# One piece of expert weights as nine DMAs instead of one: three w_down pieces at the end of a two-layer encoder

## The reference

```python
def swiglu(t, w_gate, w_up, w_down):
    return (jax.nn.silu(t @ w_gate) * (t @ w_up)) @ w_down

def moe_swiglu(h, w_router, w_gate, w_up, w_down):
    ...
    for e in range(N_EXPERTS):
        ye = swiglu(t, w_gate[e], w_up[e], w_down[e]).astype(jnp.float32)
        out = out + gates[:, e:e + 1] * ye
```

## Time and profile before

| | |
|---|---|
| three executions | 1026.13, 1026.95, 1029.49 us; median 1026.95 us |
| the profiled execution | 1027.61 us |
| its span, first to last instruction | 1024.7 us |
| granted TensorE clock, mean | 0.995 of full speed |
| TensorE busy | 1005.4 us, 98% |
| DMA queue q1 (SP) | 331.64 MB, 82.8% of 16 engines' span |

### The profile page before, as it was taken

How to read it: one execution, slowest core, us unless ns; L and a number is a source line. 1 busy time by engine, 2 the same in 40 slices (tenths; PEclk the granted TensorE clock), 3 DMA queues, 4 the chain that set the end, 5 groups by cost and what they waited for, 6 DMA issues and landing times.

```text
span 1024.7 us, 22739 instructions
## 1 busy us (share of the span) xinstructions
PE 1005.4 (98%) x10130; PEld 572.4 (56%) x10130; DVE 268.6 (26%) x420; ACT 246.2 (24%) x424; POOL 33.7 (3%) x120
## 2 busy tenths in 40 slices
PE   8999999999999899999999999999999999999995
PEld 8987888888898744533334444444444444444331
DVE  7677455554857610000000000000000000000022
ACT  7667434353866200001000000000000000000121
POOL 4000000000101000000000000000000000000010
PEclk9999999999999999999999999999999999999998
DMA  8577665653447999999999999999999999999994
GB/s 282 193 257 250 202 205 168 201 175 111 154 166 289 389 408 419 408 417 418 408 419 416 408 419 415 419 409 416 418 409 419 404 419 409 408 397 418 417 418 167
DMA packets 125744, 346.88 MB, mean 339 GB/s; under 512 B 7224, under 2 KB 42848, under 8 KB 125648
## 3 DMA queue, kind: packets, MB, share of 16 engines
q1 hardware_dynamic: 119632, 331.64, 82.8%
q0 software_dynamic: 3008, 10.40, 3.1%
q10 hardware_dynamic: 3008, 3.42, 0.9%
HBM read 340.71 MB, written 4.72 MB: 337 GB/s over the span
## 4 chain that ended last, share of the span: by engine, by line
PE 90%; DMA 4%; ACT 2%; SPq 2%; DVE 2%; issue 1%; DVEq 0%; ACTq 0%
PE ps L2060 28%; PE ps L2123 14%; PE ps L2071 11%; PE ps L1592 8%; PE ps L1594 8%; PE ps L1593 8%; PE ps L2128 6%; DMA ring<-in_moe_w_down 2%; PE ps L2081 1%; DMA raw_gu<-in_w_out 1%; SPq L885 1%; DMA raw_gu<-in_w_in 1%; PE ps L2157 1%; PE ps L1599 1%; SPq L791 0%
## 5 line engine op out<-in xcount | busy, mean ns | idle before, releaser
L2060 PE MATMUL ps<-ring,xg 128*32 128x512 f32 (+2 forms) x2736 | 315.1, 551 | 0.6 <-ACT xg L1493 0.6
L2123 PE MATMUL ps<-ring,moe_ht 128*32 128x512 f32 x1184 | 149.4, 593 | 1.4 <-DMA ring<-in_moe_w_down 1.4
L2071 PE MATMUL ps<-ring,xg 128*32 128x256 f32 (+2 forms) x2064 | 147.1, 357 | 0.0
L2071 PEld LDWEIGHTS ps<-ring,xg 128*32 128x32 f32 x2064 | 67.1, 110 | 131.4 <-issue 128.6
L2060 PEld LDWEIGHTS ps<-ring,xg 128*32 128x32 f32 x2736 | 86.3, 110 | 77.2 <-issue 44.1
L1592 PE MATMUL ps<-hi_gu,xt_hi 128*128 128x512 f32 (+1 forms) x336 | 125.8, 374 | 0.8 <-DVE lo_gu L2315 0.7
L1594 PE MATMUL ps<-hi_gu,xt_lo 128*128 128x512 f32 (+1 forms) x336 | 123.2, 367 | 0.0
L1593 PE MATMUL ps<-lo_gu,xt_hi 128*128 128x512 f32 (+1 forms) x336 | 123.0, 366 | 0.0
L1475 ACT ACTIVATE moe_silu<-ps 128x512 f32<-128x512 f32 (+2 forms) x24 | 13.4, 557 | 332.4 <-PE ps L2071 274.2
L2770 DVE TENSOR_TENSOR moe_hidden<-moe_silu,ps 128x512 f32<-128x512 f32 (+2 forms) x24 | 15.3, 638 | 242.6 <-PE ps L2071 142.8
L1592 PEld LDWEIGHTS ps<-hi_gu,xt_hi 128*128 128x128 f32 x336 | 63.8, 190 | 12.3 <-issue 1.8
(11 more groups left out here) (345 smaller groups left out, 966.3 us busy)
## 6 DMA issues: line engine op xcount, KB each, us to landing
ring<-in_moe_w_down SPq DMA_DIRECT2D x74, 1024.0 KB, 17.4
ring<-in_moe_w_up SPq DMA_DIRECT2D x59, 1024.0 KB, 17.7
ring<-in_moe_w_gate SPq DMA_DIRECT2D x57, 1024.0 KB, 16.6
ring<-in_moe_w_gate SPq DMA_DIRECT2D x27, 768.0 KB, 17.4
ring<-in_moe_w_up SPq DMA_DIRECT2D x24, 768.0 KB, 14.5
raw_gu<-in_dense_w_gate SPq DMA_DIRECT2D x22, 512.0 KB, 3.9
raw_gu<-in_dense_w_up SPq DMA_DIRECT2D x22, 512.0 KB, 4.8
raw_d<-in_dense_w_down SPq DMA_DIRECT2D x11, 1024.0 KB, 4.9
```

The costliest lines, as they stand in the source:

```text
L2060: last = pe.matmul(ps[tile(q), (B_GATE, B_UP)[part], 0:w // 2], xg[:, rows_at, k, tile(g)], weights[:, h * w // 2:(h + 1) * w // 2], start ...
L2071: last = pe.matmul(out, xg[:, rows_at, k, A_SLOTS:SLOTS], own, start=k == 0, stop=k == KT - 1)
L2123: last = pe.matmul(ps[tile(q), B_YA, :], moe_ht[:, at:at + 32], weights[:, h * 512:(h + 1) * 512], start=start, stop=stop)
```

## The change

Of the four DOWN pieces of chunk 1 of the last expert the first three, D0 to D2, are loaded as nine DMAs each: one of the partitions 64 to 127, all 64 of them, and eight of eight partitions each, which are every fourth partition of 0 to 31 and then of 32 to 63 (0, 4, ... 28; 1, 5, ... 29; and so on). The bytes, their places in HBM and in SBUF, and the order of the pieces stay. Each of the nine DMAs adds 16 to the slot's semaphore, so `FILL` counts nine loads for such a piece and the level that `down` waits for rises by 144 in place of 16. The path for more tokens than the slots hold (`step` not None) keeps its single DMAs; its levels are counted on from the new ones.

```diff
+BY_EIGHT = 64
...
+    def loads_of(p, c, part, i):
+        return 1 + BY_EIGHT // 8 if (p, c, part) == (E - 1, CHUNKS - 2, DOWN) and i < 3 else 1
...
-        FILL.append(SLOT.count(slot) + 1)
+        FILL.append(sum(loads_of(*key) for key, at in zip(PIECE, SLOT) if at == slot) + loads_of(p, c, part, i))
...
-        fills = SLOT.count(slot)
+        fills = max(f for f, at in zip(FILL, SLOT) if at == slot)
...
-                    sp.dma_start(ring_at(slot).rearrange("p (k n) -> p k n", k=2),
-                                 expert_rows(moe_w_down, e)[r0:r0 + FC, :].rearrange("(k p) n -> p k n", p=P)
-                                 ).then_inc(ring_loaded[slot], 16)
+                    to = ring_at(slot).rearrange("p (k n) -> p k n", k=2)
+                    rows_of = expert_rows(moe_w_down, e)[r0:r0 + FC, :].rearrange("(k p) n -> p k n", p=P)
+                    if step is None and loads_of(p, c, part, i) > 1:
+                        sp.dma_start(to[BY_EIGHT:P], rows_of[BY_EIGHT:P]).then_inc(ring_loaded[slot], 16)
+                        for j in range(BY_EIGHT // 8):
+                            some = slice(j // 4 * 32 + j % 4, (j // 4 + 1) * 32, 4)
+                            sp.dma_start(to[some], rows_of[some]).then_inc(ring_loaded[slot], 16)
+                    else:
+                        sp.dma_start(to, rows_of).then_inc(ring_loaded[slot], 16)
```

## The result

| | before | after |
|---|---|---|
| executions | 5 | 5 |
| time, us | 1026.13 to 1029.49, median 1027.59 | 1037.09 to 1039.09, median 1038.16 |
| the profiled execution, us | 1027.61 | 1037.09 |
| its span, us; mean clock | 1024.7; 0.995 | 1035.1; 0.989 |

The ratio is 1.0105 with the 95% interval [1.0094, 1.0115]. Costs in us are worked out from ratios in what follows, as (ratio - 1) x 1027; the change's is 10.8 us. I had forecast 1028.3 us, at most 1030.9, and a time that can't be told from the one before as the likeliest answer. The prediction was wrong.

A forecast was written before the change was run, and what follows sets the result against it. The landings of pieces D0 to E2, not the matmuls, were taken to set the end. Issue 0, semaphore writes 0 and transfer +1.4 us on a median of 1026.95 gave 1028.3 us, range 1025.1 to 1030.9.

The forecast's parts named there:

- Cost 0, upper bound 1 us: SP's 27 issues for D0 to D2: 20 us, D3 issued about 996, hidden by the queue's cover; cost 0, at most 1 us.
- 1.7 us of cover: D3, issued at 996, could land by 1001.3 and is wanted at 1003.0: 1.7 us to spare.
- my own floor of 5.3 us for D3: Least time from D3's issue on an idle queue to landing: 2.48 us of transfer and 2.8 us of a tiny load.
- +1.4: Transfer of D0 to D2: the half ahead ends 7.4 us later with 6.0 us of lead, so E2 lands 1.4 us later.
- The lagging half stays at 1010.4: Transfer: the lagging engines save bytes but lose pace on the shared upper partitions, so their end does not move.
- its slack of 1.5 us: Last up piece: lands at 993.0, used at 994.54; D0's contention of 1.24 us doesn't use up the 1.5 us.
- with 6.0 us of lead: End of the DMAs: eight of sixteen engines end about 6 us before the other eight, read from the falling DMA share.
- the half that gets more is the half ahead: Assumed for the sum: the engines given more bytes by the eights are those ahead; no row names the half.
- rival C: The half that gets more is behind; pieces from D2 on land up to 3.7 us later: 1030.7 us; chance 0.18.
- Rival A: An engine's own rate limits and the half ahead gets more: 1.8 us earlier, 1025.1 us; chance 0.25.
- Rival D: The eights spread over all engines, or the issue hides all: no shift, 1027.0 us; chance 0.10.
- paid nothing twice: E0 to E2: a delay at D3 runs through turning and adding to E0 as well and is not paid twice.

The follow-up runs named there:

- e5: DMAs alone, no computation: whole pieces, upper halves, halves in turn, eights; SP needed 19.6 us for three pieces in the change's form.
- e2: Kernel before, with D0 to D2 whole, each followed by eight tiny DMAs of eight partitions into an unread buffer: 1034.26 us, ratio 1.0066.
- e12: The change with other partitions, against the kernel before: the DMA of 64 takes the odd ones, the eights the even ones: 1034.60 us, ratio 1.0067.
- e9: Kernel before, with D0 to D2 each loaded as two DMAs, odd 64 and even 64 partitions: 1026.23 us, ratio 0.9995.
- e1: Kernel before, with D0 to D2 each loaded as two DMAs, upper 64 and lower 64 partitions: 1040.66 us, ratio 1.0133.
- e3: The change on D0 alone, against the kernel before: 1031.31 us, ratio 1.0047.
- e7: e2 on D0 alone, one whole DMA and eight tiny ones, against the kernel before: 1026.50 us, ratio 0.9992.
- e8: e1 on D0 alone, upper 64 and lower 64 partitions, against the kernel before: 1031.94 us, ratio 1.0040.
- e6: Kernel before plus a tiny DMA of eight partitions and a marker behind E2, run once for its trace: six completions by 1003.3, two at 1009.1 and 1009.5.
- e11: Kernel before plus tiny DMAs of four and six partitions with markers behind E2, run once for its trace: the four complete 6.7 us ahead of E2.
- e10: DMAs alone, no computation, by choice of partitions: contiguous halves 208 or 209 GB/s, every second partition 413; tiny DMAs of 8 issued in 0.27 to 0.33 us.

## Why the prediction was wrong

**Issue, "Cost 0, upper bound 1 us": the step that failed first.** I forecast 20 us for the three pieces and D3 at 996; it took 29.2 and was 1006.40. The 10.4 us between are: 24 x (0.89 - 0.75) = 3.4 for the pitch; 4.8 for stalls of the first piece, whose first three issues took 3.92, 1.77 and 1.12 us where 0.65 and 0.70 are the unstalled ones; 1.2 because they began at 977.18 and not at 975.93; and about 1 for the three of 64 partitions and gaps. My price was 0.75 in a range of 0.5 to 0.8, the measured 0.89 lies outside it: 0.70 for the issue, where rows 7 had 0.62, and 0.19 of register work and gaps. The 20 us themselves are what e5 needed (19.6), with fixed addresses and issues that didn't stall. In the kernel the price was applied to a queue that I had myself called full, and there the small issues were stalled as well as the large. And the margin was thin: 1.7 us of cover, against an error of 10.4. Priced from the measured 29.2 us and my own floor of 5.3 us for D3, the step gives 1011.7 for a piece wanted at 1003.0, +8.7; e2 and e12, which hold this mechanism without sharing, cost 6.8 and 6.9 us (1.0066 and 1.0067). (At 0.8 us my own sum gives 996.8 for D3's issue and not 997.3; nothing hangs on it.)

**The transfer term, "+1.4", was mis-sized though its mechanism was right.** I chose the reading that the receiving side limits, and the bench fits that: 209 GB/s to a contiguous half against 413. The Trainium skill (SBUF — State Buffer, "Door 1: The DMA port swizzle") has it so: either contiguous half of the partitions is reached by 8 of the 16 ports. The runs agree, e9 against e1 above all. But I let it cost only the half of the engines that is ahead and wrote "The lagging half stays at 1010.4". By that reasoning one piece, D0, costs nothing, since its 2.5 us lie within the lead of 6.0; e3 cost 4.8 us with one piece where issue costs nothing (e7), and e8, in which no engine has more bytes than before, 4.1 (1.0040). That D0's contention, priced at 1.24 us, would leave the last up piece within its slack of 1.5 us failed too: in the change that piece was used as soon as it landed, at 997.79, 4.8 us later than the 993.0 of before. When a whole DMA goes to one side, the other side's capacity stands unused: at 209 GB/s a piece of 1 MB takes 5.0 us, not 2.5, which is 2.5 us more for each piece, 7.5 for three. e1 lost more than that, 13.7: between 985 and 1010 e1 moved 5 x (271 + 234 + 219 + 229 + 233) = 5930 KB at this rate, though only 3 MB are in halves. Up pieces that share the engines with the halves were slowed as well, as their waits show. That the two halves of the engines, out of step by 6 us, make these stretches overlap, is my argument for the surplus; no run parts it (e5, with nothing else under way, has just the halving: 220 GB/s).

**"with 6.0 us of lead", the half that gets more is the half ahead: not true for all of it.** Six of the eight engines are ahead and two are behind (e6), so a part of rival C was in the change from the start. How much it costs by itself isn't measured. It is little beside the others: e12 has this unequal load as the change does, e2 has none of it, and they are equal within their intervals, which are some 2.5 us to either side.

**How the two causes share the 10.8 us.** They don't add. Issue alone is 1.0066, sharing alone 1.0133, both 1.0105. Taking sharing out of the change (e12) brings 1.0105 to 1.0067, some 3.9 us by the ratios; the profiled executions, by the start of E2 (1020.76 and 1019.28), say 1.5. So of the loss about 7 us would be there by issue alone, and 1.5 to 4 us come from sharing on top, neither known to better than about 2 us. The windows tell why there is so little on top: in e12 the engines stand idle where the change has them busy at half pace (from 995 to 1005 a share of 0.51 and 0.42 for 158 and 131 GB/s, against 0.76 and 0.69 for twice 184). Slow bytes fill time that late issues would have left empty. For one piece it is the other way round: issue costs nothing (e7), transfer all of it (e3, e8).

**What held.** A DMA of eight partitions runs on eight engines: e6 and e11 agree with it, and in the changed trace each new piece's semaphore gets 88 completions from the engines, 16 + 8 x 9 (eight engines and one by the queue itself), where sixteen engines for each would have given 9 x 16 = 144 or more. The Trainium skill (DMA: Bandwidth & Descriptors, "Why a DMA increments its semaphore by 16 and not by 1") gives this count of engines. Rival A is out, since an engine's own rate isn't the limit. Rival D, no shift, is out too. E0 to E2 paid nothing twice, as I had said: E0 follows D3 by the same 4.17 us as before. (In e2 and e12, whose queue is late by issue alone, TensorE waited for E2 once more, 0.85 and 0.51 us.)

**What became of the lag.** The change was to let the half that is behind end earlier, and in one way it did: fifteen of D3's sixteen completions came from 1010.95 to 1011.67 and the last at 1013.09, no longer in two groups of eight. But e2, which moves no load between the engines, has D3's sixteen within 0.3 us (1010.03 to 1010.31). So it needs no balancing: in both kernels the engines had stood without work for part of 995 to 1010, and the half that was behind could catch up. In e1, whose engines are never idle before 1010, the two groups are still there (eight by 1005.4, the last at 1015.5). The lag vanished because time was lost, and none was won by it.

**The clock.** The granted clock fell to 0.69 and 0.63 from 1000 to 1010, behind TensorE's wait of 4.16 us, and D0 and D1 took 6.29 us together, against 1.90 + 1.92 before; 0.50 in a window of e2 is the lower of the two levels, 1.2 GHz. It didn't set the end: D2 was still waited for by 0.92 us.

**What stays open.** What makes eight engines lag by 6 us in the kernel before was not tested. Nor was the reading of HBM parted from the receiving side, as said at e10. I didn't try moving load only off the engines that lag, through DMAs of four partitions for the others: by e6 and e11 that is the choice of engines which a change of this aim would need, but 64 partitions in fours are sixteen issues, twice as many as here for a piece, at a time when eight are too many. No version that I ran is faster than the kernel before by more than its scatter (e7 and e9 are within 0.1%).

## What to carry to other kernels

Before splitting a DMA to balance engines, multiply the number of pieces by the pitch at which the queue issues them, stalls of a full queue included, and compare with the pitch at which the data is used: here 8 x 0.89 us for 1 MB against 2.48 us, which the cover here bears once and not three times (D3's issue could slip from 986.2 to 997.7, 11.5 us). When a DMA must be of 64 partitions, let it take every second one; a contiguous half ran at half the rate here, and slowed the pieces under way with it (e8). A busy share near 1 doesn't say that the throughput is full: read the GB/s beside it.

## What the runs showed of the hardware

- One contiguous half of the partitions receives 208 to 209 GB/s from sixteen busy engines; all 128, or odd and even ones in turn, 413.
- In company, that is worse than its own arithmetic: three pieces in halves cost 13.7 us (interval 11.9 to 15.4) where 7.5 were to be expected. One piece cost 4.1 where it was 2.5, which its interval of 2.0 to 6.3 doesn't part.
- An issue of eight strided partitions takes 0.70 us with a pitch of 0.89, longer than one of 128 partitions (0.37 us) of sixteen times the bytes. It isn't the count alone: in e10, 16-byte pieces of partitions 0 to 7, at a fixed address, were issued in 0.27 to 0.33 us. It isn't the address or the bytes either: e5's strided eights of 64 KB at fixed addresses took 0.67 us (pitch 0.72), e2's strided ones of 16 bytes a partition 0.70. That leaves the stride of four partitions, which no run changes by itself.
- After some 670 us of nearly full load eight of sixteen engines were 6 us behind the others, and level with them again once all had stood idle in part (e2): two among the eight that serve a DMA of eight partitions, none among the four of a DMA of four.
